# The group loop of a state-space layer: a re-ordered scan, with work moved from VectorE and GpSimd to ScalarE and back

## The chip, the cores and the metric

The kernel runs on one core of a Trainium2 chip. The metric is the device time of one execution in microseconds (us). Engines are named as in the profile: PE (TensorE), DVE (VectorE), ACT (ScalarE), POOL (GpSimd), SP (SyncE, which here only issues DMAs).

## What is computed

Two blocks of two layers each, in fp32, over 512 tokens of width 1024. Only the first layer, a Mamba-2 mixer, is touched. Per group g of 8 (4 heads of 64 each, state 128), cut to what matters:

```
z, xbc, dt = split(h @ w_in)                    # per group: 6 tiles of 128 columns
xbc = silu(conv4(xbc) + bias)                   # causal, 4 taps, per channel: x (2 tiles), B, C
for each chunk c of 128 tokens (4 chunks), head r (4 heads):
    decay = exp(min(a_cs[l] - a_cs[s], 0)), lower triangle     # a_cs: running sum of dt * A
    y  = ((C B^T) * decay) @ (x * dt)                          # inside the chunk
    y += (C * exp(a_cs)) @ state                               # from earlier chunks
    state = state * exp(a_cs[-1]) + B^T (x * dt * exp(a_cs[-1] - a_cs))
y = (y + D * x) * silu(z);   y = rmsnorm(y) @ w_out
```

## The kernel before

The whole stage lies in `ssm` (from L708). Every engine has its own queue, written out by hand; order on an engine is program order, and engines meet only at semaphores. Each product of the input projection ("piece" p of group i, L274) is 24 matmuls of 128x128 by 512 columns: 8 slices of the contraction, each in three parts, because a weight tile is split in a high part (ACT, L233, `high`) and a low part (DVE, L249, `low_on_vector`). Three split tiles are kept, so `high` and `low` run three pieces ahead.

A step i projects group i and scans group i-1. On PE (L817 on) it is: piece 0, prep 0; piece 1, out 0, prep 1; piece 2, out 1, prep 2; piece 3, out 2, prep 3; piece 4, out 3; piece 5. `prep` (L781) transposes x and B of a chunk (L789) and makes C B^T (L792). `out` (L798) makes y (L804, and L806 from the state for chunks 1 to 3) and the new state contribution (L810). A piece p waits until the result of piece p-2 has been taken out of PSUM (`lin_free`).

ACT takes pieces 0 to 3 out by a copy (L842) and pieces 4 and 5, the gates z, by Silu (L845) into `zs`; the Silu of a gate waits until the gate products of the group before (L983) are done, since `zs` is one buffer. Per chunk it copies B (L851), takes the exponential of the decay distances (L853) and, for chunks 1 to 3, of the prefix (L857). At the head of a step it does four Silus of the convolved tiles (L864).

DVE per chunk: x * dt (L947), mask of C B^T (L950), x for the state (L952), four decay distances (L956), then it waits for ACT's exponential and multiplies (L960, tile `ssm_m`); then the convolution of one tile of group i (first tap with bias L934, three taps L936), a low part (L249), and the state update (L967, L970 or, for chunk 0, L973). After chunk 3 and another low part, `gate` (L977): L981, L982, and L983, a copy to `wide`, twice. `Steps.settle` is a wait of an engine on its own last result. In the hardware loop (groups 2 to 6) such a wait is against a register.

POOL: C times exp(prefix) (L893, tile `ssm_cs`), the squares of the gated tiles (L899) and their sum (L901). SP refills the weight slots after each low part, and the prefix rows (L754) of a chunk after the chunk of the group before has used them.

After step 8, which only scans, the next block begins on PE with the sum of squares over partitions (L525).

## Time and profile before

| | |
|---|---|
| median of 3 runs | 2572.05 us (2561.34 to 2572.7) |
| profiled execution | 2570.96 us, of which span of the core 2569.0 us |
| mean granted TensorE clock | 0.930 of 2.4 GHz |
| busy, whole span | PE 89%, DVE 58%, ACT 38%, POOL 6% |
| the SSM stage (steps 0 to 8) | from about 35 us to 477 us of the span |

The profile is one execution. A line of a timeline gives start, duration, engine, source line, operation and operands, and in brackets the idle time of the engine before it and who ended it. Operations of one engine overlap by about 0.1 us, so the cost of one in a row is the difference of two starts, a little less than its duration.

### The profile page before, as it was taken

What the parts mean: (1) busy time and instruction counts of PE and PEld (TensorE: products, weight loads), DVE (VectorE), ACT (ScalarE), POOL (GpSimd) and SP (SyncE); (2) the same over time, 40 slices, a digit from 0 to 9 for tenths busy, and PEclk for the clock granted to TensorE, in tenths of its full rate; (3) what the DMA queues carried; (4) which work ended last, traced back from release to release, by engine and by line L of the source; (5) the groups of instructions that cost most, each with busy time, mean ns of one, the idle gap of its engine ahead of it and who ended that gap; (6) DMA issues with size and microseconds to landing.
All of it is one profiled execution on the core that took longest, in us unless ns stands there. A gap on an engine that the chain in (4) does not pass through costs nothing. (4 is left out here: it accounts for less than half of the span.)

```text
span 2569.0 us, 41123 instructions
## 1 busy us (share of the span) xinstructions
PE 2277.5 (89%) x15376; PEld 1969.5 (77%) x15376; DVE 1487.9 (58%) x2535; ACT 984.0 (38%) x1799; POOL 146.5 (6%) x100
## 2 busy tenths in 40 slices
PE   5988887597997779998999999989788869999998
PEld 4766665385665568885999999977666649999997
DVE  5867776635444456664566663359745445666622
ACT  4433333324444334554444432224344434434322
POOL 1021111100000000000000000022211100000000
PEclk7999998798999789997999999988999969999999
DMA  4532221133320111120233333311101102333331
GB/s 112 135 88 81 78 78 49 33 98 75 66 50 8 50 49 50 52 59 4 83 90 90 90 99 100 81 41 34 50 25 33 41 17 83 90 90 90 103 91 44
DMA packets 361091, 172.06 MB, mean 67 GB/s; under 512 B 67519, under 2 KB 359128, under 8 KB 361000
## 3 DMA queue, kind: packets, MB, share of 16 engines
q1 hardware_dynamic: 360616, 170.28, 24.1%
q0 software_dynamic: 384, 0.58, 0.2%
q8 instruction: 55, 0.90, 0.1%
q14 instruction: 36, 0.29, 0.0%
HBM read 168.68 MB, written 2.16 MB: 67 GB/s over the span
## 5 line engine op out<-in xcount | busy, mean ns | idle before, releaser
L274 PE MATMUL ps<-h_parts,parts 128*128 128x264 f32 (+1 forms) x8672 | 1353.0, 315 | 53.2 <-ACT wide L845 23.1
L274 PEld LDWEIGHTS ps<-h_parts,parts 128*128 128x128 f32 x8672 | 1208.0, 192 | 156.9 <-issue 32.3
L233 ACT ACTIVATE parts<-ring 128x1024 fp32r<-128x1024 f32 (+1 forms) x286 | 311.3, 1093 | 791.5 <-PE ps L274 544.0
L249 DVE TENSOR_TENSOR parts<-ring,parts 128x1024 fp32r<-128x1024 f32 (+1 forms) x257 | 329.5, 1288 | 251.3 <-ACT parts L233 251.1
L274 PE MATMUL ps<-wide_parts,parts 128*128 128x264 f32 (+1 forms) x1152 | 350.7, 304 | 0.0
L274 PE MATMUL ps<-up_hidden,parts 128*128 128x264 f32 x1408 | 257.9, 285 | 1.8 <-PEq L2135 1.8
L274 PEld LDWEIGHTS ps<-wide_parts,parts 128*128 128x128 f32 x1152 | 219.4, 190 | 8.0
L274 PEld LDWEIGHTS ps<-up_hidden,parts 128*128 128x128 f32 x1408 | 217.9, 188 | 2.1 <-issue 2.1
L2118 DVE TENSOR_TENSOR up_u<-ps,norm_rstd 128x264 f32<-128x264 f32 x176 | 75.4, 429 | 162.6 <-PE ps L274 155.2
L241 POOL TENSOR_TENSOR parts<-ring,parts 128x1024 fp32r<-128x1024 f32 x29 | 69.4, 2397 | 1482.2 <-ACT parts L233 1482.2
L1563 PE MATMUL ps<-wide 64*128 64x256 f32 (+5 forms) x384 | 77.3, 487 | 23.0 <-ACT wide L1700 15.8
L274 PE MATMUL ps<-gated_high,parts 128*128 128x512 f32 x256 | 85.2, 406 | 9.2 <-DVE wide_parts L298 8.2
L2385 DVE TENSOR_TENSOR res<-ps,res 128x264 f32<-128x264 f32 (+1 forms) x64 | 27.4, 432 | 102.9 <-PE ps L274 96.5
L936 DVE SCALAR_TENSOR_TENSOR ssm_conv<-wide,vec,ssm_conv 128x512 f32<-128x512 f32 x96 | 72.1, 752 | 10.1 <-DVE ssm_conv L936 0.8
L1819 DVE TENSOR_REDUCE dsa_mx<-ps 128x1 f32<-128x128 f32 (+4 forms) x80 | 42.6, 532 | 60.1 <-PE ps L1566 58.7
L2128 DVE SCALAR_TENSOR_TENSOR up_hidden_plain<-up_u,vec,up_hidden_plain 128x528 f32<-128x528 f32 x88 | 67.7, 769 | 10.3 <-DVE up_hidden_plain L2126 2.8
L2105 ACT ACTIVATE up_hidden_plain<-up_u,vec 128x528 f32<-128x528 f32 x88 | 71.7, 815 | 0.0
L274 PEld LDWEIGHTS ps<-gated_high,parts 128*128 128x128 f32 x256 | 48.8, 190 | 27.6 <-DVE wide_parts L298 8.2
L1700 ACT ACTIVATE wide<-ps,dsa_nm 128x128 f32<-128x128 f32 (+4 forms) x80 | 44.1, 556 | 65.9 <-DVE dsa_nm L1820 65.9
L1681 ACT ACTIVATE wide<-ps 128x264 f32<-128x264 f32 x80 | 31.1, 389 | 98.5 <-PE ps L274 71.0
L2126 DVE SCALAR_TENSOR_TENSOR up_hidden_plain<-up_u,vec,up_hidden_plain 128x528 f32<-128x528 f32 x88 | 66.9, 761 | 0.0
L1563 PEld LDWEIGHTS ps<-wide 64*128 64x128 f32 (+1 forms) x384 | 25.6, 166 | 48.9 <-ACT wide L1700 21.7
(294 smaller groups left out, 2549.5 us busy)
## 6 DMA issues: line engine op xcount, KB each, us to landing
ring<-in_ffn_w_up SPq DMA_DIRECT2D x88, 512.0 KB, 3.7
ring<-in_ssm_w_in SPq DMA_DIRECT2D x48, 512.0 KB, 3.9
ring<-in_ffn_w_down SPq DMA_DIRECT2D x32, 704.0 KB, 4.5
ring<-in_att_w_in SPq DMA_DIRECT2D x48, 256.0 KB, 3.6
ring<-in_da_w_qkv SPq DMA_DIRECT2D x24, 512.0 KB, 3.7
ring<-in_dsa_w_in SPq DMA_DIRECT2D x24, 512.0 KB, 3.7
ssm_prefix<-prefix_rows SPq DMA_DIRECT2D x32, 256.0 KB, 3.3
ring<-in_ssm_w_out SPq DMA_DIRECT2D x16, 512.0 KB, 4.1
```

Source lines behind the costliest of these rows:

```text
L233: self.nc.scalar.activation(self.part(st, u, 0), self.slot(u, st.kt), ACT.Copy).then_inc(self.w_high, 1)
L241: self.nc.gpsimd.tensor_tensor(self.part(st, u, 1), self.slot(u, st.kt), self.part(st, u, 0).bitcast(F32), ALU.subtract).then_inc(self.w_l ...
L249: self.nc.vector.tensor_tensor(self.part(st, u, 1), self.slot(u, st.kt), self.part(st, u, 0).bitcast(F32), ALU.subtract).then_inc(self.w_l ...
L274: m = self.nc.tensor.matmul(out, w[:, n], b, start=start and f == j == 0, stop=stop and f == st.kt - 1 and j == 2)
L936: ins = v.scalar_tensor_tensor(acc, u[:, q, j:j + SEQ], k.col(V_CW + 32 * j + tile), acc, ALU.mult, ALU.add)
L1563: m = nc.tensor.matmul(S[0:nq, x, lo:hi], rop[h, 0, c:N], rop[h, 1, lo:hi], start=True, stop=not masked)
L1700: nc.scalar.activation(p[0:nq, x, 0:c + nq], S[0:nq, x, 0:c + nq], ACT.Exp, bias=nm[0:nq, x:x + 1], scale=0.125, accum_out=den[0:nq, x:x + ...
L1819: do(v.reduce_max(mx[0:nq, x:x + 1], S[0:nq, x, 0:N], AX.X))
L2105: nc.scalar.activation(cc[:, x, :], u[:, x, 0:T2], ACT.Identity, scale=k.col(w0 + t), bias=k.col(w2 + 2 * FT + t)).then_inc(s_tap, 1)
L2118: v.tensor_tensor(u[:, x, 2 + b * HALF:2 + (b + 1) * HALF], ps[:, 2 + (2 * x + b) % 4, 0:HALF], k.rstd[:, b * HALF:(b + 1) * HALF], ALU.mu ...
L2126: v.scalar_tensor_tensor(acc, u[:, x, 1:1 + T2], k.col(w0 + 2 * FT + t), acc, ALU.mult, ALU.add).then_inc(s_mid, 1)
L2128: v.scalar_tensor_tensor(acc, u[:, x, 2:2 + T2], k.col(w2 + t), acc, ALU.mult, ALU.add).then_inc(s_conv, 1)
```

## The change

- The decay distances (`distances`) of chunk c+1 are made on DVE at the end of chunk c, those of chunk 0 at the head of the step; their exponentials and those of the prefix (`decay`, in `chunk`) follow on ACT one chunk early.
- C times exp(prefix) moves from POOL to DVE, after `ssm_m`. The state update of chunk c-1 (`carry`) moves into chunk c, between the mask and x for the state.
- The first tap of the convolution moves from DVE to ACT (`tap`), with scale and bias as columns.
- The squares move from POOL to ACT, their sum from POOL to DVE (`add_squares`), one step later; POOL has nothing left in the stage.
- `gate` writes its product straight to `wide`; the copy is gone, and `yg` is one buffer.
- ACT: `keep` copies first and then makes the high part; the gate z0 is taken out at the end of a step and waits only for the first gate product of the group before; z1 is taken out at the head of the next step; the four Silus are made at the end of the step.
- DVE: the gate follows the low part of slot 4 at once; one low part is after it, one at the head of the next step.

```diff
@@ scalar
+                def keep(i, p):
+                    act.wait_ge(sem["lin_done"], 6 * i + p + 1)
+                    wait(act, sem["conv"], 4 * i - 3 + p if not isinstance(i, int) or i else 0)
+                    nc.scalar.activation(u[:, p, 3:3 + SEQ], ps[:, p % 2, :], ACT.Copy).then_inc(sem["lin_free"], 1)
                     k.high(act, st, st.after(i, p, st.depth))
+                def tap(i, p):
+                    tile = tile_of(i, p)
+                    act.wait_ge(sem["lin_free"], 6 * i + p + 1)
+                    nc.scalar.activation(cw[:, p, :], u[:, p, 0:SEQ], ACT.Identity, scale=k.col(V_CW + tile),
+                                         bias=k.col(V_CB + tile)).then_inc(sem["tap"], 1)
+                def gates_in(i, j):
+                    act.wait_ge(sem["lin_done"], 6 * i + 5 + j)
+                    k.high(act, st, st.after(i, 4 + j, st.depth))
+                    wait(act, sem["gate"], 2 * i - 1 + j if not isinstance(i, int) or i else 0)
+                    nc.scalar.activation(zs[:, j, :], ps[:, j, :], ACT.Silu).then_inc(sem["lin_free"], 1)
+                def squares(s):
+                    for j in range(2):
+                        act.wait_ge(sem["gate"], 2 * s + j + 1)
+                        wait(act, n["accumulated"], 2 * s + b_acc + j)
+                        nc.scalar.activation(sqg[:, j, :], gated(s, j), ACT.Square).then_inc(n["squared"], 1)
+                def decay(s, c):
+                    act.wait_ge(sem["seg"], 4 * s + c + 1)
+                    nc.scalar.activation(seg[:], seg[:], ACT.Exp).then_inc(sem["dec"], 1)
                 def chunk(s, c):
+                    act.wait_ge(sem["xt"], 4 * s + c + 1)
+                    wait(act, sem["y"], 4 * s + c)
                     nc.scalar.activation(bt[:], TR[:, 2 * P:3 * P], ACT.Copy).then_inc(sem["bt"], 1)
+                    if c < CHUNKS - 1:
+                        decay(s, c + 1)
+                        wait(act, sem["cs"], 3 * s + c)
+                        act.wait_ge(s_bc[c + 1], 16 * s + 16)
+                        nc.scalar.activation(ebc[:], bc[:, c + 1], ACT.Exp).then_inc(sem["ebc"], 1)
                 def step(i, lin=True, scan=True):
                     if scan:
+                        gates_in(i - 1, 1)
+                        decay(i - 1, 0)
+                    for p in range(1, 5):
                         if lin:
+                            keep(i, p - 1)
...
+                        if lin:
+                            tap(i, p - 1)
+                        if scan:
+                            chunk(i - 1, p - 1)
+                    if lin:
+                        gates_in(i, 0)
+                        silus(i)
+                    if scan:
+                        squares(i - 1)
@@ vector, chunk
                     v.tensor_tensor(cbm[:], CB[:, 0:P], k.tri, ALU.mult).then_inc(sem["cbm"], 1)
+                    if c:
+                        carry(s, c - 1)
...
-                    dve.wait_ge(s_bc[c], 16 * s + 16)
-                    for r in range(RPG):
-                        ins = v.tensor_scalar(seg[:, r, :], bc[:, c, r, :], scal(1, c, r), 0.0, ALU.subtract, ALU.min)
-                    ins.then_inc(sem["seg"], 1)
                     dve.wait_ge(sem["dec"], n + 1)
                     dve.wait_ge(sem["cbm"], n + 1)
                     v.tensor_tensor(mm[:], seg[:], cbm[:].unsqueeze(1).to_broadcast([P, RPG, P]), ALU.mult).then_inc(sem["m"], 1)
+                    if c:
+                        dve.wait_ge(sem["ebc"], 3 * s + c)
+                        v.tensor_tensor(cs[:], ebc[:], cv[:, 3:4, c * P:(c + 1) * P].to_broadcast([P, RPG, P]), ALU.mult).then_inc(sem["cs"], 1)
+                    if c < CHUNKS - 1:
+                        dve.wait_ge(sem["m"], n + 1)
+                        distances(s, c + 1)
@@ vector, gate
                     for j in range(2):
-                        do(v.tensor_tensor(yg[:, j, :], yg[:, j, :], zs[:, j, :], ALU.mult))
-                        v.tensor_copy(k.wide[:, bass.ds(2 * s + j, 1), 0:SEQ].rearrange("p a t -> p (a t)"), yg[:, j, :]).then_inc(sem["gate"], 1)
+                        wait(dve, sem["gate"], 2 * s + j)
+                        do(v.scalar_tensor_tensor(yg[:], cv[:, j, :], k.dexp[:, bass.ds(2 * s + j, 1)], Y[j], ALU.mult, ALU.add))
+                        v.tensor_tensor(gated(s, j), yg[:], zs[:, j, :], ALU.mult).then_inc(sem["gate"], 1)
@@ vector, step
+                        distances(i - 1, 0)
+                        if lin:
+                            k.low_on_vector(dve, st, (i, 2))
+                        if squares:
+                            add_squares(i - 2)
+                    for p in range(1, 5):
                         if scan:
+                            chunk(i - 1, p - 1)
                         if lin:
+                            conv(i, p - 1)
+                            if scan or p >= 3:
+                                k.low_on_vector(dve, st, st.after(i, p - 1, st.depth))
                     if scan:
                         gate(i - 1)
                         steps.end()
                     if lin:
+                        conv_steps.end()
+                        k.low_on_vector(dve, st, st.after(i, 4, st.depth))
```

## Rows read from the trace of the kernel before

**Rows 1.** Engines in one step: stretch, length, busy (count), PE clock, DMA share, GB/s
```profile
235.00:284.00 49.00, 43.18 (x226) 33.83 (x225) 37.05 (x66) 18.07 (x28) 7.22 (x7) 0.97 0.31 85
```
**Rows 2.** Waits of PE in steps 1 to 7: total us, times, longest
```profile
PE ps L274 <- ACT wide L845: 23.1, 6, 3.9
PE ps L804 <- POOL ssm_cs L893: 21.4, 19, 1.6
```
**Rows 3.** Timeline of PE, one step: start, us, operation, [idle before]
```profile
234.72 7.38 PE L274 MATMUL ps<-h_parts,parts 128*128 128x512 f32 x24 [3.91 <-ACT wide L845]
241.94 0.49 PE L789 MATMUL ps<-cst,ssm_xbc 128*128 128x128 f32 x3
...
242.41 5.81 PE L274 MATMUL ps<-h_parts,parts 128*128 128x512 f32 x24
248.15 0.66 PE L804 MATMUL ps<-ssm_m,ssm_xdt 128*64 128x128 f32 x8
...
249.74 5.81 PE L274 MATMUL ps<-h_parts,parts 128*128 128x512 f32 x24
255.96 0.45 PE L804 MATMUL ps<-ssm_m,ssm_xdt 128*64 128x128 f32 x4 [0.40 <-POOL ssm_cs L893]
...
258.01 5.81 PE L274 MATMUL ps<-h_parts,parts 128*128 128x512 f32 x24
...
274.83 0.45 PE L804 MATMUL ps<-ssm_m,ssm_xdt 128*64 128x128 f32 x4 [1.57 <-POOL ssm_cs L893]
...
275.88 5.85 PE L274 MATMUL ps<-h_parts,parts 128*128 128x512 f32 x24
285.64 4.60 PE L274 MATMUL ps<-h_parts,parts 128*128 128x512 f32 x12 [3.91 <-ACT wide L845]
```
**Rows 4.** Windows behind such a wait, columns as in Rows 1
```profile
288.00:290.00 2.00, 2.00 (x6) 1.63 (x5) 0.63 (x2) 1.10 (x3) 0.00 (x0) 0.50 0.04 11
```
**Rows 5.** Timeline of ACT at the turn of the step
```profile
284.99 0.60 ACT L845 ACTIVATE wide<-ps 128x512 f32<-128x512 f32 x1 [9.34 <-DVE wide L983]
```
**Rows 6.** Timeline of DVE: one chunk, and the gate at the step's end
```profile
260.90 0.42 DVE L947 TENSOR_TENSOR ssm_xdt<-ps,ssm_group 128x256 f32<-128x256 f32 x1 [0.19 <-DVE ssm_state L970]
...
261.77 0.87 DVE L956 TENSOR_SCALAR ssm_seg<-ssm_prefix,ssm_group 128x128 f32<-128x128 f32 x4
263.34 0.69 DVE L960 TENSOR_TENSOR ssm_m<-ssm_seg,ssm_cb 128x512 f32<-128x512 f32 x1 [0.70 <-ACT ssm_seg L853]
...
265.68 2.54 DVE L936 SCALAR_TENSOR_TENSOR ssm_conv<-wide,vec,ssm_conv 128x512 f32<-128x512 f32 x3
268.14 1.22 DVE L249 TENSOR_TENSOR parts<-ring,parts 128x1024 fp32r<-128x1024 f32 x1
...
270.34 0.42 DVE L947 TENSOR_TENSOR ssm_xdt<-ps,ssm_group 128x256 f32<-128x256 f32 x1 [0.19 <-DVE ssm_state L970]
...
279.85 0.74 DVE L981 SCALAR_TENSOR_TENSOR ssm_yg<-ssm_xbc,dexp,ps 128x512 f32<-128x512 f32 x1
...
283.69 1.26 DVE L983 COPY wide<-ssm_yg 128x512 f32 x1
```
**Rows 7.** First tap, one line's instructions: durations in ns, min/median/max
```profile
L934 DVE TENSOR_SCALAR ssm_conv<-wide,vec x32: 541/1555/1623, 70.3 to 425.1; 128x512 f32<-128x512 f32 x32
```
**Rows 8.** The same kind of tap on ACT, in the feed-forward layer
```profile
L2105 ACT ACTIVATE up_hidden_plain<-up_u,vec x88: 809/815/820, 1282.5 to 2421.1; 128x528 f32<-128x528 f32 x88
```
**Rows 9.** Table loads of ACT in front of the exponentials, durations in ns
```profile
L853 ACT ACT_TABLE_LOAD  x8: 1283/1283/1283, 93.2 to 440.3; - x8
```
**Rows 10.** Timeline of PE before step 1 (second half is piece 0)
```profile
80.09 11.39 PE L274 MATMUL ps<-h_parts,parts 128*128 128x512 f32 x48 [1.12 <-DVE parts L249]
```
**Rows 11.** Timeline of PE in step 8 (scan only) and at the next block
```profile
438.54 0.90 PE L789 MATMUL ps<-cst,ssm_xbc 128*128 128x128 f32 x3 [5.15 <-ACT ssm_xbc L864]
...
450.76 0.70 PE L804 MATMUL ps<-ssm_m,ssm_xdt 128*64 128x128 f32 x4 [4.43 <-POOL ssm_cs L893]
...
477.30 2.04 PE L525 MATMUL ps<-norm_acc,cst 128*128 128x512 f32 x2 [8.08 <-PEq L742]
```

More of the change, by code:

```diff
@@ new lines, in gates_in, with silus @@
+                def gates_in(i, j):
[3 more added lines that the diff above has]
+                    nc.scalar.activation(zs[:, j, :], ps[:, j, :], ACT.Silu).then_inc(sem["lin_free"], 1)
+                def silus(s):
+                    wait(act, sem["gate"], 2 * s)
+                    for q in (2, 3, 0, 1):
+                        act.wait_ge(sem["conv"], 4 * s + q + 1)
+                        nc.scalar.activation(cv[:, q, :], cw[:, q, :], ACT.Silu).then_inc(sem["silu"], 1)
@@ L847, in chunk @@
                 def chunk(s, c):
-                    n = 4 * s + c
-                    act.wait_ge(sem["xt"], n + 1)
-                    wait(act, sem["y"], n)
+                    act.wait_ge(sem["xt"], 4 * s + c + 1)
+                    wait(act, sem["y"], 4 * s + c)
                     nc.scalar.activation(bt[:], TR[:, 2 * P:3 * P], ACT.Copy).then_inc(sem["bt"], 1)
-                    act.wait_ge(sem["seg"], n + 1)
-                    nc.scalar.activation(seg[:], seg[:], ACT.Exp).then_inc(sem["dec"], 1)
@@ L859, in step @@
                 def step(i, lin=True, scan=True):
                     if scan:
-                        wait(act, sem["gate"], 2 * (i - 1))
-                        for q in (2, 3, 0, 1):
-                            act.wait_ge(sem["conv"], 4 * (i - 1) + q + 1)
-                            nc.scalar.activation(cv[:, q, :], cw[:, q, :], ACT.Silu).then_inc(sem["silu"], 1)
-                    for p in range(6):
+                        gates_in(i - 1, 1)
+                        decay(i - 1, 0)
@@ L880, in _ @@
                 tables.act(act)
+                act.wait_ge(sem["group"], 1)
                 step(0, scan=False)
@@ L937, in conv, with distances @@
                         if j < 3:
-                            do(ins)
+                            conv_steps.mark(ins)
+                            conv_steps.settle(dve)
                         else:
                             ins.then_inc(sem["conv"], 1)
+                def distances(s, c):
+                    dve.wait_ge(s_bc[c], 16 * s + 16)
+                    for r in range(RPG):
+                        ins = v.tensor_scalar(seg[:, r, :], bc[:, c, r, :], scal(1, c, r), 0.0, ALU.subtract, ALU.min)
+                    ins.then_inc(sem["seg"], 1)
                 def chunk(s, c):
@@ L1018, in _ @@
                 step(0, scan=False)
-                step(1)
+                step(1, squares=False)
                 with dve.Fori(2, GROUPS - 1) as i:
```

105 lines of the change are left out of this document (25 added, 80 removed).

## The prediction

> **What bounds the kernel now.** I read the table of engines by stretch first: in one step of the loop PE is busy 43.2 of 49 us, DVE 37.1, ACT 18.1 [rows 1]. So PE is the first suspect, but not alone. The table of waits shows where it stands still: in steps 1 to 7 there are six waits of 3.9 us for the Silu that takes a gate out of PSUM, and nineteen, of up to 1.6 us, for C times decay from POOL [rows 2]. The timeline of PE then gives the step: 285.64 - 234.72 = **50.92 us**, start to start [rows 3]. The window behind the long wait shows the granted clock at 0.50, that is 1.2 GHz, in a stretch in which PE had just stood idle [rows 4], and piece 0 takes 7.22 us start to start where the others take 5.74 (248.15 - 242.41) [rows 3]: 1.5 us more per long wait.
>
> Who holds PE up? At the turn, the Silu L845 waits 9.34 us for the copy L983 at the end of DVE's gate [rows 5]. The gate lasts from 279.85 to 284.95, 5.1 us [rows 6], with the last copy stretched to 1.26 us. Inside the step DVE goes from one L947 to the next in 270.34 - 260.90 = **9.44 us**, with only 0.70 + 0.19 us idle [rows 6]. So DVE sets the pace of a chunk, and PE's wait for POOL is the shadow of it.
>
> **PE's floor.** Without its waits a step on PE is, start to start [rows 3]: slot 0, 5.74 + 0.47 (241.94 to 242.41) = 6.21; slot 1, 249.74 - 242.41 = 7.33; slots 2 and 3, 5.74 + 2.05 (255.96 to 258.01) = 7.79 each; slot 4, 5.74 + 1.05 (274.83 to 275.88) = 6.79; piece 5, 5.74. Sum **41.65 us**, 9.27 less than now. The change touches nothing on PE but a wait already met.
>
> **The new DVE slot,** c = 2, from start differences [rows 6]. Stays: L947, L950, L952, 0.87 (260.90 to 261.77). State update moved in: 270.34 - 268.14 less the low part's 1.13 = 1.07, less the settling wait of 0.19 that goes = 0.88. `ssm_m`: 0.69 less the overlap with the next, 0.61. C times decay is new here; the nearest row is `ssm_m` itself, same shape and operands, 0.61 to 0.69; I take 0.65. Distances of c+1: 0.87, I take 0.90. Three taps 265.68 to 268.14, 2.46. Low part 1.13. Sum **7.5 us** against 9.44. Gone are the first tap (265.68 - 263.34 - 0.61 = 1.73; its durations go from 0.54 to 1.62, long when POOL works beside it [rows 7]) and the wait for the exponential, 0.70. That is under PE's 7.79. It need not even be: the distance from PE's transposes to the C times decay they lead to is 0.87 + 0.88 + 0.61 + 0.69 + about 0.1 = 3.15 us, and PE has a piece of 5.74 to do meanwhile, so DVE may be 2.6 us late before PE waits.
>
> **ACT in a slot:** copy 0.5, high part 1.0, tap, B 0.3, two exponentials 1.2. The tap's price on ACT is read from the feed-forward layer: 0.815 us for 528 columns, with two column operands [rows 8]; 0.8 here. Bounds: 0.6 (ACT's plain pass, L845, [rows 5]) and 0.82. Total about 3.8 us of 7.79. The tap is queued in front of B, the exponentials and, on DVE, the three taps with a low part behind them. ACT begins it about 1.6 us after a piece ends; DVE comes to it only after the transposes (2.05) and 4.0 us of its own. So I cost it at nothing; with that cover gone it would cost 0.8 per slot, 22 us in 28 slots.
>
> On one page the rule goes against this. The Trainium skill, "ScalarE: Activation LUTs", section "Rules for kernel authors", says to put multiplies and adds on VectorE rather than ScalarE. The rows agree on the size (0.54 undisturbed against 0.8), and the sum by the rule would have the tap cost DVE 0.54 more per slot, 8.0 us, which is over PE's slot but inside DVE's lateness allowance; either way my sum stays.
>
> **The turn of the step.** Count from T, the end of piece 4. out 3 ends at T + 1.05. DVE has done its taps by then, and its low part, by T + 0.8. Gate without copies: 0.78 + 0.73, twice, plus settling: first product at T + 2.7, second at T + 4.2. The Silu of z0 needs only the first: T + 3.3. The next piece 0 starts at T + 1.05 + 5.74 = T + 6.79, so the 3.91 us wait goes with 3.5 us to spare, and with it the slow piece 0. What is late next: the low part of piece 2, at the head of the step. Its high part follows piece 5 and the squares on ACT: T + 6.8, or after four Silus (2.2) and two squares (1.2 to 1.3) behind the gate, T + 7.7, so high at T + 8.7, low at T + 9.9, two additions (0.7 each, with settling 1.7) T + 11.6. DVE's chunk 0 can begin when the transposes come, T + 6.79 + 6.1 = T + 12.9. Slack 1.3 us, and slot 0 has 1.8 more (DVE 5.7, PE 7.33). If Silu and Square called for more table loads, up to 2.6 us [rows 9], slot 0 would swallow it.
>
> DMAs: SP's queue keeps its order; each prefix refill waits for events that come earlier or in the same slot, and refills stay a group ahead. The same bytes in 42 us instead of 51 make about 100 GB/s where 85 is seen [rows 1]. Nothing; above zero would be one late weight tile of the order of the 3.9 us wait.
>
> **The sum.** Steps 1 to 7 run from the start of piece 0, 80.09 + 5.7 = 85.8 [rows 10], to 433.4 (438.54 less 5.15 [rows 11]): 347.6 us. Seven floors are 291.6. I add 0.3 us per step for hand-overs that I don't see, between 0 and 1.5 as bounds: 293.7. Gain **53.9** (45 to 56).
>
> Before step 1: the 1.12 us wait for the low part of piece 5 [rows 10] goes, since three first taps leave DVE ahead of it, 1.1.
>
> Step 8 has no pieces to hide behind; here the chain counts [rows 11]. The 5.15 us wait for the Silus goes, as they are made before piece 5 ends; instead the first exponential (z1 0.6, table load 1.3 [rows 9], Exp 0.7, `ssm_m` 0.75) comes 3.4 to 3.6 after piece 5, where `out` 0 is now 9.6 after it: 6.0. Three waits of about 4.4 hold distances, two exponentials and POOL's 1.3 one behind another; the new chain, x to C times decay, is 2.7 for chunk 1 and 3.2 for chunks 2 and 3 instead of 4.8 to 4.4: 2.0 + 1.2 + 1.2 = 4.4. From y to the next block is 8.08; new: gate 3.05, square 0.7, addition 0.8, end of block 0.5 = 5.05: 3.0. Gain **13.4** (9 to 15).
>
> In all 68.4 us. Against the profiled execution, 2570.96, it makes 2502.6; the median is 1.1 above that execution, so **2504 us**.
>
> **The rivals.**
> *DVE stays the pacemaker.* Register waits on an own result cost some 0.15 each in the loop (0.19 before L947 [rows 6]); if the new order has more of them than I count, or DVE waits for ACT's tap, a DVE slot of 8.7 makes PE late by 0.9 in three slots, 2.7 per step: + 19, 2523 us. For it: DVE's 7.5 is only 0.3 under PE's. Against: 2.6 us of lateness are allowed and the turn gives back 1.3.
> *The turn stays.* If the first gate product comes over 3.5 us later than I say, PE still waits up to 3.9 and runs at 1.2 GHz after it. 5.4 of 9.3 us per step stay: + 35, 2539 us.
> *Hand-over in series, the slower side.* ACT and DVE now feed each other twice per slot (distances to exponential, tap to taps). If neither runs ahead, a slot is 7.5 + 3.8 = 11.3 instead of 9.44, and the gate stays last: 4 x 1.9 less 1.7 for the copies = 5.9 per step, + 41, less the tail's 13: 2599 us. It decides once ACT reaches the tap over 4 us late. Against it: the one wait of this kind now is 0.70, and it lies in front of work that is moved ahead of it.
> *No visible change:* a new wait of 8 us per step in the place of the old ones, for instance a weight tile that lands late now that steps are shorter, near 2565 us.
>
> **How the numbers follow.** Forecast 0.70 (2494 to 2512), pacemaker 0.15 (2512 to 2530), turn 0.07 (2530 to 2559), no change 0.04, slower 0.04. The range 2493 to 2532 takes in the first two: about 0.85. Within 0.5% is what a measurement of this kernel can't tell from no change: faster 0.92, same 0.04, slower 0.04.
>
> **What would show it.** Right: PE steps of 41.7 to 42.5 us start to start, granted clock 1.0 throughout steps 2 to 7, no PE wait for L845's successor nor for C times decay; DVE idle at the head of the step, before the transposes; step 8 and gate to the next block in about 30 us (PE from piece 5's end to L525: 30.5 instead of 43.9). Wrong: PE waiting for `ssm_cs` or `ssm_m` in slots 2 to 4 (pacemaker), a window at clock 0.5 in each step (turn), DVE waiting for `tap` or `dec` (series), ACT's high part waiting for DMA.

## The result, and the profile after

The changed kernel takes 2489.78 us (median of 4 runs, 2486.38 to 2496.44) against 2571.77 us (2561.34 to 2572.7) for the kernel before in the same comparison: ratio 0.9693, interval [0.9661, 0.9726]. The forecast was 2504 us, in a range of 2493 to 2532. The sign was right. The time is 3.2 us under the low end: 82.0 us were gained where about 68 had been forecast.

The profiled execution took 2486.38 us. The head of its page:

```profile
span 2484.3 us, 41025 instructions
...
PE 2250.7 (91%) x15376; PEld 1952.1 (79%) x15376; DVE 1452.3 (58%) x2528; ACT 1014.6 (41%) x1847; POOL 75.5 (3%) x43
```

The next view answers to [rows 1]: engines in a whole step of the loop (stretch, length, busy and count of PE, weight loads, DVE, ACT and POOL, granted clock, DMA share, GB/s).

```profile
244.88:286.38 41.50, 41.50 (x229) 33.02 (x227) 33.03 (x65) 22.85 (x36) 0.00 (x0) 1.00 0.37 101
```

A step is now 41.50 us long, PE is busy in all of it, at a granted clock of 1.00 (2.4 GHz). Before, it was 43.2 of 49. The waits of PE in the whole stage answer to [rows 2] (total us, times, longest). None lies in steps 1 to 7:

```profile
PE ps L808 <- DVE ssm_cs L967: 7.9, 3, 2.8
...
PE ps L525 <- PEq L748: 5.0, 1, 5.0
PE ps L808 <- DVE ssm_m L964: 3.4, 1, 3.4
```

The timeline of PE answers to [rows 3]: two pieces back to back at the turn of the step (x48), then slot by slot; no bracket is left.

```profile
244.88 11.40 PE L274 MATMUL ps<-h_parts,parts 128*128 128x512 f32 x48
256.12 0.49 PE L793 MATMUL ps<-cst,ssm_xbc 128*128 128x128 f32 x3
...
279.09 0.49 PE L793 MATMUL ps<-cst,ssm_xbc 128*128 128x128 f32 x3
...
286.38 3.99 PE L274 MATMUL ps<-h_parts,parts 128*128 128x512 f32 x16
```

DVE answers to [rows 6]: one chunk, then the gate at the turn, the head of the step and the next chunk 0.

```profile
271.80 0.42 DVE L953 TENSOR_TENSOR ssm_xdt<-ps,ssm_group 128x256 f32<-128x256 f32 x1 [0.96 <-PE ps L793]
...
273.46 0.68 DVE L964 TENSOR_TENSOR ssm_m<-ssm_seg,ssm_cb 128x512 f32<-128x512 f32 x1
274.06 0.68 DVE L967 TENSOR_TENSOR ssm_cs<-ssm_ebc,ssm_xbc 128x512 f32<-128x512 f32 x1
...
275.45 2.53 DVE L934 SCALAR_TENSOR_TENSOR ssm_conv<-wide,vec,ssm_conv 128x512 f32<-128x512 f32 x3
277.90 1.22 DVE L249 TENSOR_TENSOR parts<-ring,parts 128x1024 fp32r<-128x1024 f32 x1
279.62 0.42 DVE L953 TENSOR_TENSOR ssm_xdt<-ps,ssm_group 128x256 f32<-128x256 f32 x1 [0.50 <-PE ps L793]
...
287.67 0.69 DVE L988 TENSOR_TENSOR wide<-ssm_yg,wide 128x512 f32 x1
...
294.41 1.23 DVE L249 TENSOR_TENSOR parts<-ring,parts 128x1024 fp32r<-128x1024 f32 x1 [2.07 <-ACT parts L233]
295.56 1.50 DVE L993 TENSOR_TENSOR norm_acc<-norm_acc,ssm_squares 128x512 f32<-128x512 f32 x2
298.14 0.42 DVE L953 TENSOR_TENSOR ssm_xdt<-ps,ssm_group 128x256 f32<-128x256 f32 x1 [1.09 <-PE ps L793]
```

The roles have changed: before each chunk DVE now waits for PE's transposes. ACT at the same turn answers to [rows 5]; the wait of 9.34 us for the gate is 0.63:

```profile
288.40 0.60 ACT L860 ACTIVATE wide<-ps 128x512 f32<-128x512 f32 x1 [0.63 <-DVE wide L988]
```

PE in step 8 and at the next block answers to [rows 11]:

```profile
375.06 0.54 PE L793 MATMUL ps<-cst,ssm_xbc 128*128 128x128 f32 x3
...
379.25 1.12 PE L808 MATMUL ps<-ssm_m,ssm_xdt 128*64 128x128 f32 x8 [3.42 <-DVE ssm_m L964]
...
384.93 0.45 PE L808 MATMUL ps<-ssm_m,ssm_xdt 128*64 128x128 f32 x4 [2.34 <-DVE ssm_cs L967]
...
397.99 0.70 PE L808 MATMUL ps<-ssm_m,ssm_xdt 128*64 128x128 f32 x4 [2.80 <-DVE ssm_cs L967]
...
404.99 2.04 PE L525 MATMUL ps<-norm_acc,cst 128*128 128x512 f32 x2 [5.01 <-PEq L748]
```

**Where the time went.** Three landmarks of PE's timeline cut the span: the first projection matmul of the stage, L525 (the next block's first use of the sum of squares), and the end. Before: 37.4, 477.3 and 2569.0; after: 36.1, 405.0 and 2484.3. So the start gave 1.3 us (it lies between 35.8 and 37.3 us in all the traces of this document, whatever the kernel), the stage went from 439.9 to 368.9 (**71.0 us**), and everything behind L525, in which no instruction was changed, went from 2091.7 to 2079.3 (**12.4 us**). The forecast had 68.4 for the stage and no term at all for what lies behind it.

Behind L525, the segments between further landmarks agree within half a microsecond, but for two: the sliding-window attention layer (from the end of the state-space layer's output projection to the last product with V) went from 277.5 to 271.6, the sparse attention layer from 397.4 to 390.8. In windows of the sliding-window layer laid at the same work (583 before is 511 after), first before, then after:

```profile
629.00:675.00 46.00, 44.09 (x191) 33.68 (x191) 18.30 (x26) 16.86 (x34) 0.00 (x0) 0.96 0.35 77
675.00:721.00 46.00, 42.09 (x232) 30.94 (x231) 22.43 (x35) 21.05 (x41) 0.00 (x0) 0.95 0.24 52
721.00:767.00 46.00, 44.08 (x236) 32.40 (x235) 20.70 (x34) 21.05 (x51) 0.00 (x0) 0.94 0.22 56
```

```profile
557.00:603.00 46.00, 44.09 (x198) 33.89 (x197) 19.47 (x29) 17.12 (x36) 0.00 (x0) 1.00 0.37 81
603.00:649.00 46.00, 42.09 (x240) 31.31 (x239) 22.30 (x36) 21.86 (x45) 0.00 (x0) 1.00 0.27 58
649.00:695.00 46.00, 44.08 (x248) 32.77 (x247) 22.88 (x35) 21.21 (x44) 0.00 (x0) 1.00 0.21 58
```

PE is busy for the same time and gets 27 more matmuls done, since the clock is 1.00 instead of 0.94 to 0.96. 46 us at 0.95 lose 2.3 us against 1.00, so three such windows would account for the 5.9 us of this layer and a little more. The sparse layer shows the same, first two windows of before, then the same work after:

```profile
1914.00:1964.00 50.00, 42.87 (x338) 33.19 (x337) 23.04 (x51) 21.96 (x58) 7.10 (x3) 0.96 0.11 31
1964.00:2014.00 50.00, 42.71 (x342) 32.96 (x342) 25.60 (x54) 19.56 (x58) 7.10 (x3) 0.93 0.10 25
```

```profile
1836.00:1886.00 50.00, 42.37 (x359) 32.48 (x356) 24.38 (x53) 22.00 (x60) 7.09 (x3) 1.00 0.12 31
1886.00:1936.00 50.00, 42.36 (x350) 32.13 (x349) 26.80 (x59) 21.22 (x62) 7.11 (x3) 1.00 0.11 31
```

### The profile page after: what moved, and what is told of

The parts are those of the page before. It is cut to its first block and busy times, and to the rows that moved or that the text cites. A ratio compares the mean times of both kernels' runs of the same rounds, so it can differ in the third digit from the quotient of the medians.

```text
span 2484.3 us, 41025 instructions
## 1 busy us (share of the span) xinstructions
PE 2250.7 (91%) x15376; PEld 1952.1 (79%) x15376; DVE 1452.3 (58%) x2528; ACT 1014.6 (41%) x1847; POOL 75.5 (3%) x43
## 5 line engine op out<-in xcount | busy, mean ns | idle before, releaser
L274 PE MATMUL ps<-h_parts,parts 128*128 128x264 f32 (+1 forms) x8672 | 1335.6, 312 | 28.8 <-DVE h_parts L298 16.4
L274 PEld LDWEIGHTS ps<-h_parts,parts 128*128 128x128 f32 x8672 | 1195.6, 190 | 127.0 <-issue 30.9
L274 PEld LDWEIGHTS ps<-gated_high,parts 128*128 128x128 f32 x256 | 49.0, 191 | 27.2 <-DVE wide_parts L298 7.8
```

Of the source, the lines that this page charges most:

```text
L274: m = self.nc.tensor.matmul(out, w[:, n], b, start=start and f == j == 0, stop=stop and f == st.kt - 1 and j == 2)
```

## The experiments

Two questions were open: why unchanged layers ran faster, and whether the parts of the stage's sum hold one by one. "Stage" is from the first projection matmul to L525 in the profiled execution; "outside" is the median less the stage, in which all runs count. "Sliding" and "sparse" are the two attention layers in the profiled execution. The kernel before and the changed kernel, measured first, have 439.9 and 368.9, 2131.9 and 2120.9, 277.5 and 271.6, 397.4 and 390.8 in the last four columns. All times are in us. The experiments were measured in three groups, on different chips, each beside fresh runs of the kernel before, so ratios compare better across groups than medians.

| kernel | median (n) | ratio to before | stage | outside | sliding | sparse |
|---|---|---|---|---|---|---|
| before_again | 2569.25 (10) | 0.9994 [0.9979, 1.0009] | 440.6 | 2128.7 | 277.6 | 396.8 |
| after_again | 2488.52 (4) | 0.9671 [0.9647, 0.9695] | 368.7 | 2119.8 | 275.4 | 390.8 |
| delay1 | 2495.42 (5) | 0.9705 [0.9693, 0.9718] | 369.6 | 2125.8 | 277.6 | 400.9 |
| delay4 | 2497.81 (4) | 0.9710 [0.9687, 0.9733] | 370.6 | 2127.2 | 275.8 | 396.9 |
| delay8 | 2497.91 (4) | 0.9713 [0.9689, 0.9736] | 374.3 | 2123.6 | 273.1 | 393.8 |
| before_delay | 2577.80 (11) | 1.0029 [1.0019, 1.0039] | 445.2 | 2132.6 | 277.0 | 400.0 |
| only_turn | 2529.29 (4) | 0.9842 [0.9826, 0.9859] | 401.9 | 2127.4 | 274.5 | 396.8 |
| only_tap | 2551.92 (4) | 0.9930 [0.9913, 0.9947] | 423.4 | 2128.5 | 275.5 | 396.9 |
| tap_on_vector | 2498.77 (4) | 0.9729 [0.9713, 0.9745] | 369.3 | 2129.4 | 277.0 | 394.2 |
| late_decay | 2501.15 (4) | 0.9734 [0.9718, 0.9751] | 375.9 | 2125.2 | 275.9 | 396.9 |
| cs_on_gpsimd | 2493.39 (4) | 0.9698 [0.9683, 0.9712] | 366.3 | 2127.1 | 277.7 | 396.7 |
| short_tail | 2488.66 (5) | 0.9693 [0.9677, 0.9708] | 364.7 | 2123.9 | 277.4 | 390.8 |

### The same kernels again, and the next block later

before_again and after_again are the two kernels unchanged.

> The kernel before, once more, for a second trace of it. The stage that was changed ended 72.3 us earlier in the changed kernel, but the whole span was 84.7 us shorter; 12.4 us came out of layers whose code is the same. Theory A (clock by chance): those layers take a different time from one execution to the next, since the same idle gaps of PE of about 1.9 us are followed by a stretch at 1.2 GHz in one execution and not in the other. Then this trace has the changed stage at 441 us after the first projection matmul to L525 to within 1 us (477.3 less 37.4 is 439.9), but the sliding-window layer and the sparse-attention layer differ from the first trace by some us, in steps of about 1.7. Theory B (a steady gain of the change): both layers take the same time as in the first trace to within 0.5 us, 2091.7 us from L525 to the end.

> The changed kernel, once more. Both theories: ratio 0.966 to 0.973. Theory A (clock by chance behind the stage): from L525 to the end of the span 2079 us in the first trace, here anything from 2079 to 2092, while the stage itself repeats to within 1 us (404.99 less 36.1 is 368.9). Theory B (steady gain): 2079.3 to within 1 us.

Both came back: 2569.25 (2566.68 to 2571.68) and 2488.52 (2484.69 to 2490.46). The part behind L525 was 2091.9 and 2083.0. So the extra gain is no accident of one execution; it came again with this kernel, 9 to 12 us of it by the profiles. But it is not one fixed pattern either: the kernel before repeated its two layers within 0.6 us, about as theory B had it, while in the changed kernel the sliding-window layer took 271.6 in one execution and 275.4 in another.

delay4 and delay8 put four and eight settled memsets on DVE at the end of the stage, in front of the next block. Nothing else changes; all layers behind start that much later.

```diff
                 add_squares(GROUPS - 1)
+                late = Steps(k.sem("ssm_late"))
+                for _ in range(4):
+                    late.mark(v.memset(yg[:], 0.0))
+                    late.settle(dve)
```

> The changed kernel with four dummy writes of the gate buffer on DVE, each waiting for itself, behind the last sum of squares: L525 comes 1.5 to 2 us later and nothing else is touched. Theory A (where PE's gaps fall decides the clock): the rest of the span differs from 2079.3 by up to some us either way, in the sliding-window and sparse-attention layers, with episodes at 1.2 GHz of the same length after the same gaps in some iterations and not in others. Theory B: the rest is 2079.3 and the median grows by 1.5 to 2 us.

> The same with eight dummy writes: L525 comes 3 to 4 us later. Theory A: the rest again moves by some us either way and not in proportion to the delay. Theory B: the median grows by 3 to 4 us against the changed kernel.

PE's wait in front of L525 grew from 5.01 us to 7.64 and 10.28, 0.66 us for each memset. The stage became 1.9 and 5.6 us longer than in after_again, the median 9.3 and 9.4 us. (The stage of delay4 would be 1.5 us longer but for its first part: the profiled execution had no slow stretch ahead of step 1; see "Before step 1" below.) The time outside the stage therefore rose by 7.4 and by 3.8 us, without an instruction changed there; behind L525 the profiled executions took 2090.1 and 2083.9 us, where after_again has 2083.0. Four more memsets left the median where it was. That speaks against a steady gain behind the stage and for grants that hang on when the layers run. One pair of lines shows what differs: the same place in the sliding-window layer, where PE stands idle for 1.92 us until ACT has stored the transposed scores. First before, then after:

```profile
699.50 1.90 PE L1319 MATMUL ps<-swa_pt,swa_v 128*64 128x128 f32 x16 [1.92 <-ACT swa_pt L1382]
701.33 2.81 PE L1277 MATMUL ps<-swa_raw,cst 128*128 128x512 f32 x4
```

```profile
625.67 1.09 PE L1333 MATMUL ps<-swa_pt,swa_v 128*64 128x128 f32 x16 [1.92 <-ACT swa_pt L1396]
626.69 1.98 PE L1291 MATMUL ps<-swa_raw,cst 128*128 128x512 f32 x4
```

The idle time is equal to the hundredth. Behind it the 16 matmuls take 1.90 us in one kernel and 1.09 in the other: the one is at 1.2 GHz there, the other at 2.4.

The clock records of the traces allow a count of such stretches in the middle of the sliding-window layer, from 40 to 220 us behind its start. The changed kernel's first trace has none, and the layer took 271.6 us; delay8 has one (273.1); only_turn, after_again and only_tap have two (274.5 to 275.5); delay4, late_decay, before_delay and tap_on_vector three (275.8 to 277.0); the kernel before in both traces, delay1, short_tail and cs_on_gpsimd four (277.4 to 277.7). So the differences of this layer are slow stretches that came or stayed away, and the two executions of the changed kernel differ by two of them.

delay1 has one memset, to see how little is enough. before_delay puts ten on the kernel before: if only the changed kernel were sensitive, it should cost the delay and no more.

```diff
                 step(GROUPS, lin=False)
+                late = Steps(k.sem("ssm_late"))
+                for _ in range(10):
+                    late.mark(v.memset(mm[:], 0.0))
+                    late.settle(dve)
```

> The changed kernel with one dummy write: L525 0.5 us later. Theory A: the time outside the stage depends on where the layers behind it fall to within a fraction of a microsecond (0.5 us of a longer stage in tap_on_vector went with + 9 us outside it): anything from 2120 to 2130, not 2120.5 necessarily. Theory C (what matters is the work in the stage, DVE's load above all): 2120 to 2121.

> The kernel before with ten dummy writes of ssm_m's buffer on DVE behind the last gate; the first five or six hide behind POOL's squares, so L525 comes 1.5 to 2.5 us later and the stage is 442 to 443 us. Theory A (where the later layers' gaps fall decides the clock): the time outside the stage, 2129 us in the kernel before, moves by several us, either way, as it did by + 7 with a delay of 1.8 us in the changed kernel. Theory C (the change itself leaves the later layers faster, and any delay spoils it): nothing to spoil here, 2129 to within 1.5, and the median 2572.

In delay1 L525 comes 0.66 us later behind the same work, the stage is 0.9 us longer than in after_again, and the median 6.9 us (2492.21 to 2503.17, none of its five runs as fast as the slowest of after_again, though one of the first four runs of the changed kernel, 2496.44, was as slow). The two were measured in different groups, and the interval of delay1's ratio, [0.9693, 0.9718], touches after_again's and overlaps that of the first comparison, [0.9661, 0.9726]. So a cost of so small a shift is likely, not proven; delay4 and delay8, measured beside after_again, are clear of it in every run. Its profiled execution is the slowest of the five, so its columns on the right show a bad case: the sparse layer took 400.9 us. In before_delay the stage was 445.2, 5.3 us more than in the kernel before and over the 442 to 443 expected: 4.0 in step 8, and 1.3 from a slow stretch ahead of step 1. The median rose by 7.7 against its neighbours' 2570.06. So the kernel before moves too, by 2 to 3 us outside the stage, and in the costly direction, which speaks against theory C, that a delay only spoils what the change had gained.

Over all the kernels the sparse layer took 390.8, then 393.8 and 394.2, then 396.7 to 397.4, then 400.0 and 400.9 us: steps of about 3 us. Executions with the same time mostly have the same stretches at 1.2 GHz at the same places of the layer: after, after_again and short_tail to 0.1 us, and before_again, only_turn, delay4 and late_decay to 0.3. That whole slow stretches come or stay away is shown; what in the timing decides on one of them isn't.

### The turn alone

only_turn is the kernel before with the turn of the step changed: gate before the low part, the product written to `wide` without the copy, z0 released by the first gate product.

```diff
-                        wait(act, sem["gate"], 2 * i)
+                        wait(act, sem["gate"], 2 * i + p - 5 if not isinstance(i, int) or i else 0)
...
-                        do(v.tensor_tensor(yg[:, j, :], yg[:, j, :], zs[:, j, :], ALU.mult))
-                        v.tensor_copy(k.wide[:, bass.ds(2 * s + j, 1), 0:SEQ].rearrange("p a t -> p (a t)"), yg[:, j, :]).then_inc(sem["gate"], 1)
+                        v.tensor_tensor(k.wide[:, bass.ds(2 * s + j, 1), 0:SEQ].rearrange("p a t -> p (a t)"), yg[:, j, :], zs[:, j, :], ALU.mult).then_inc(sem["gate"], 1)
...
-                        k.low_on_vector(dve, st, st.after(i, 4, st.depth))
                     if scan:
                         gate(i - 1)
                         steps.end()
                     if lin:
+                        k.low_on_vector(dve, st, st.after(i, 4, st.depth))
```

> The kernel before with the turn of the step alone: the gate product is written in place (no copy), z0 waits for the first product of the group before only, and one low part goes behind the gate. Theory 'DVE's pace': chunks stay at 9.44 us and PE's waits of 1.6 us for C times decay stay, but the wait of 3.9 us for z0 and the 1.2 GHz stretch behind it go: step 45.5 us, stage 405 us. Rival: the turn wait only moves, to the low part or the Silus of the convolved tiles; step over 48, stage over 422.

The stage fell by 38.0 us, 3 more than expected. In two steps of the loop the long wait for the gate's Silu has gone, and these are all of PE's waits (total us, times, longest):

```profile
PE ps L804 <- POOL ssm_cs L893: 7.7, 5, 1.6
PE ps L789 <- DVE ssm_group L990: 0.6, 2, 0.3
```

Over steps 1 to 7 PE waits for C times decay 15 times, 19.1 us in all, and never for a gate. So over half of the 71 us lay at the turn. The waits for C times decay stay, with DVE still the pacemaker of the chunk.

### The tap alone

only_tap is the kernel before with the first tap on ACT, behind the copy that takes the piece out.

```diff
+                        act.wait_ge(sem["lin_free"], 6 * i + p + 1)
+                        nc.scalar.activation(cw[:, p, :], u[:, p, 0:SEQ], ACT.Identity, scale=k.col(V_CW + tile),
+                                             bias=k.col(V_CB + tile)).then_inc(sem["tap"], 1)
...
-                    do(v.tensor_scalar(acc, u[:, q, 0:SEQ], k.col(V_CW + tile), k.col(V_CB + tile), ALU.mult, ALU.add))
```

> The kernel before with one part alone: the first tap on ACT, right after the copy out of PSUM. Theory 'DVE's pace': a DVE chunk falls from 9.44 to 9.44 - 1.73 = 7.7 us, under PE's 7.8, so the waits for C times decay go although that product stays on POOL (chain from the transposes 4.4 us, under a piece of 5.74); the gate, still 5.1 us behind two low parts, ends at T + 7.1 where piece 0 could start at T + 6.8, so about 1 us of the wait for z0 stays and the 1.2 GHz stretch goes. Step 42.5 us instead of 50.9; the stage, from the first projection matmul to L525, 389 us where it is 440 before and 368.8 after. Rival 'the gate must be mended by itself': the wait for z0 stays at about 3.9 us with its slow piece 0, the step is 47 us and the stage 418.

This missed: the stage is 423.4 us, 16.5 less than before; the rival had 418. The forecast's 1.73 us for the first tap, taken as DVE's saving, was the error. DVE with the tap gone:

```profile
242.18 0.69 DVE L962 TENSOR_TENSOR ssm_m<-ssm_seg,ssm_cb 128x512 f32<-128x512 f32 x1 [2.75 <-ACT ssm_seg L857]
...
257.92 0.69 DVE L962 TENSOR_TENSOR ssm_m<-ssm_seg,ssm_cb 128x512 f32<-128x512 f32 x1 [0.70 <-ACT ssm_seg L857]
258.53 3.67 DVE L938 SCALAR_TENSOR_TENSOR ssm_conv<-wide,vec,ssm_conv 128x512 f32<-128x512 f32 x3
```

and POOL beside it:

```profile
258.57 1.29 POOL L897 TENSOR_TENSOR ssm_cs<-ssm_ebc,ssm_xbc 128x512 f32<-128x512 f32 x1 [6.65 <-ACT ssm_ebc L861]
267.41 1.84 POOL L897 TENSOR_TENSOR ssm_cs<-ssm_ebc,ssm_xbc 128x512 f32<-128x512 f32 x1 [7.55 <-ACT ssm_ebc L861]
```

The three taps had taken 2.54 us [rows 6]. Now they take 3.67, because POOL's product, which starts when the exponential is there, meets them instead of the first tap. 1.1 of the 1.73 us were POOL's, and they moved on to the next instruction; the tap itself is the 0.54 us that stood as the shortest in [rows 7]. A second cost is new: in slot 0 the tap stands on ACT in front of the exponential, and DVE waits 2.75 us for it, where it waits 1.70 in the kernel before. A chunk is 8.8 us (L962 to L962, 266.76 - 257.92), with 7.7 counted on, and every turn of the loop keeps a wait of 2.4 to 3.0 us for the gate (six times, 15.0 us in all), in some with a slow piece behind it. The steps are 46.9 to 48.6 us long.

The Trainium skill, "SBUF — State Buffer", section "SBUF: two separate sides", has a rule for such a size: it calls the port pair that VectorE and GpSimd share an exclusive lock, held for a whole instruction, and counts a VectorE instruction with two SBUF inputs, as these taps are, among those that need it against a GpSimd instruction that reads SBUF. The rows agree with it: 3.67 - 2.54 = 1.13, at most the length of POOL's instruction, 1.29.

In the full change the error did no harm, since POOL's product leaves together with the tap. The turn alone (38.0 us) and the tap alone (16.5) make 54.5 of the 71 us; no run combines the two without the rest.

### The tap back on DVE, in the changed kernel

tap_on_vector undoes that part alone: DVE makes the first tap again, and PE's slot has to cover it.

```diff
-                    dve.wait_ge(sem["tap"], 4 * s + q + 1)
+                    dve.wait_ge(sem["lin_free"], 6 * s + q + 1)
+                    wait(dve, sem["silu"], 4 * s)
+                    conv_steps.mark(v.tensor_scalar(acc, u[:, q, 0:SEQ], k.col(V_CW + tile), k.col(V_CB + tile), ALU.mult, ALU.add))
```

> The changed kernel with the first tap back on DVE, as the Trainium skill's page 'ScalarE: Activation LUTs' advises for multiplies and adds. Theory 'allowance': the tap takes 0.54 plus 0.15 of settling now that POOL is quiet; DVE's chunk of 7.3 to 7.8 us becomes up to 8.0, it comes some tenths late to the third and fourth transposes and PE doesn't wait, since a late DVE has 2.6 us; step 41.5, stage 369 to 370. Rival 'DVE is at its limit': every one of 28 slots costs up to 0.7 us, stage 380 to 388.

The stage is 369.3 us, 0.4 to 0.6 more than after: DVE's lateness allowance holds, as forecast. The steps are 41.50 us long in both kernels, so in the loop the place of the tap is worth nothing; the half microsecond lies in step 8 (30.5 instead of 29.9 and 29.8), which has no taps and where the stretches at 1.2 GHz fall differently. The median nevertheless rose by 9 to 10 us, nearly all of it outside the stage (2129.4, as much as in the kernel before). Someone who compared medians alone would credit the tap with 9 us; the stage shows that it brings at most half of one.

### The exponentials late again

late_decay makes distances and exponentials of chunk c in slot c, as before, with the rest of the change left in.

```diff
-                    if c < CHUNKS - 1:
-                        decay(s, c + 1)
-                        wait(act, sem["cs"], 3 * s + c)
-                        act.wait_ge(s_bc[c + 1], 16 * s + 16)
-                        nc.scalar.activation(ebc[:], bc[:, c + 1], ACT.Exp).then_inc(sem["ebc"], 1)
+                    decay(s, c)
+                    if c:
+                        wait(act, sem["cs"], 3 * s + c - 1)
+                        act.wait_ge(s_bc[c], 16 * s + 16)
+                        nc.scalar.activation(ebc[:], bc[:, c], ACT.Exp).then_inc(sem["ebc"], 1)
```

> The changed kernel with distances and exponentials back in their own chunk (distances of chunk c behind x for the state, then the exponential, ssm_m, C times decay). Theory 'allowance': the chain from the transposes to C times decay grows from 3.1 to 4.7 us, still under a piece of 5.74, so steps stay at 41.5 us; only step 8, which has no pieces, pays: 1.2 for chunk 0 and 1.6 for each of three more, stage 375 us. Rival 'one chunk early is what made the loop fast': PE waits again for C times decay, 0.3 to 1.5 us in three slots of seven steps, stage 385 to 400.

The stage is 375.9 us, 7.0 more than in the changed kernel. PE's waits in it:

```profile
PE ps L808 <- DVE ssm_cs L968: 12.7, 3, 4.4
...
PE ps L808 <- DVE ssm_m L965: 4.7, 1, 4.7
```

All four lie in step 8 (380.29, 387.54, 396.13 and 404.72): 17.4 us where the changed kernel has 11.3. In steps 1 to 7 PE waits for nothing. So the first item of the change, exponentials one chunk early, is worth nothing in the loop, with the other parts in place, and 7 us in the one step that has no pieces to hide behind.

### C times decay back on POOL

cs_on_gpsimd takes the product from DVE and gives POOL its old loop for it; the exponentials stay early.

```diff
-                    if c:
-                        dve.wait_ge(sem["ebc"], 3 * s + c)
-                        v.tensor_tensor(cs[:], ebc[:], cv[:, 3:4, c * P:(c + 1) * P].to_broadcast([P, RPG, P]), ALU.mult).then_inc(sem["cs"], 1)
...
+                def scaled_c(s, c):
+                    pool.wait_ge(sem["ebc"], 3 * s + c)
+                    wait(pool, sem["y"], 4 * s + c)
+                    nc.gpsimd.tensor_tensor(cs[:], ebc[:], cv[:, 3:4, c * P:(c + 1) * P].to_broadcast([P, RPG, P]),
+                                            ALU.mult).then_inc(sem["cs"], 1)
```

> The changed kernel with C times decay back on POOL, where its exponential is ready a chunk early, so POOL can begin as soon as PE has used the last one. Theory 'allowance': DVE loses 0.6 of its own work per chunk and gets back about 1.1 us of blocking by POOL (the same 1.27 us product made the tap 1.0 us longer before, and the three taps of only_tap up to 1.1 longer); DVE's chunk is 7.3 to 7.9 us, PE doesn't wait, step 41.5, stage 367 to 370 us. Rival 'POOL had to go': PE waits for C times decay in three slots of seven steps, stage 378 or more.

The stage is 366.3 us, 2.6 less than in the changed kernel and a little under what was expected; the median, 2493.39, is not lower. POOL can begin as soon as PE has read the last product, a slot ahead of its use:

```profile
272.36 1.29 POOL L928 TENSOR_TENSOR ssm_cs<-ssm_ebc,ssm_xbc 128x512 f32<-128x512 f32 x1 [6.53 <-PE ps L814]
```

and what it blocks on DVE meanwhile is one instruction of the state update, which takes 0.74 us instead of 0.42 and has slack beside it. The two instructions in front of it, which read PSUM, ran beside the same product in their usual 0.42 and 0.28 us:

```profile
273.18 0.74 DVE L990 TENSOR_TENSOR ssm_statet<-ssm_state,ssm_group 128x256 f32<-128x256 f32 x1
```

So with early exponentials this move to DVE wasn't needed in the loop (the steps are 41.50 us here too), and in step 8, where DVE's chain is the path, it lengthened that chain: step 8 is 27.2 us here, 29.9 in the changed kernel.

### A shorter step 8

short_tail gives step 8 an order of its own on top of the changed kernel: C times decay ahead of x * dt, the first sum of squares later, the Silu of z1 after the scan.

```diff
+                def last_chunk(s, c):
+                    n, b4 = 4 * s + c, [P, RPG, 64]
+                    if c:
+                        dve.wait_ge(sem["y"], n)
+                        scaled_c(s, c)
...
                 def chunk(s, c):
                     n, b4 = 4 * s + c, [P, RPG, 64]
+                    if isinstance(s, int) and s == GROUPS - 1:
+                        last_chunk(s, c)
+                        if c == 0:
+                            add_squares(s - 1)
+                        return
```

> The changed kernel with step 8 alone re-ordered: ACT makes the first exponential right behind the Silus and leaves the squares of group 6 and z1 until later; DVE makes C times decay before the transposes come, the decayed state at the end of the chunk before, and x for the state behind ssm_m. Loop steps stay at 41.5. The chain of step 8 loses 1.6 at its head, 0.9 in chunk 1 and 1.4 in each of chunks 2 and 3: stage 363 to 364.5 us where it is 368.8. What the time does is another matter: with the clock of the later layers as in tap_on_vector (2128 to 2130 us outside the stage) it is 2492, with that of the changed kernel (2120) 2484.

The stage is 364.7 us, 4.0 to 4.2 less and 0.2 above what was expected. That it came so near is luck: 1.5 us of the gain lie ahead of step 1, where this execution had no slow stretch. Step 8 itself fell from 29.9 to 27.3 us, by 2.6 where 5.3 had been summed. The head gained its 1.5 (a wait of 1.90 instead of 3.42), but in chunk 1 the wait grew from 2.34 to 3.99, since the sum of squares now stands in front of it on DVE:

```profile
376.73 0.66 PE L808 MATMUL ps<-ssm_m,ssm_xdt 128*64 128x128 f32 x8 [1.90 <-DVE ssm_m L981]
...
383.19 0.70 PE L808 MATMUL ps<-ssm_m,ssm_xdt 128*64 128x128 f32 x4 [3.99 <-DVE ssm_m L981]
```

The median, 2488.66 (2488.31 to 2497.16), can't be told from the changed kernel's: the 4 us were given back outside the stage (2123.9 against 2119.8 and 2120.9). No version measured here is clearly faster than the changed kernel.

## Why the prediction was wrong, point by point

**The floor of a step.** Forecast 41.65 us, plus 0.3 for hand-overs; measured 41.50, in every step of the loop and in every variant of the changed kernel. The allowance wasn't needed. Steps 1 to 7 went from 347.6 to 290.5 us, 57.1 against 53.9 forecast. The 3.2 between are the allowance (7 x 0.3 = 2.1) and seven times 0.15.

**DVE's slot.** Forecast 7.5; measured 7.82 start to start (279.62 - 271.80), of which 0.50 is idle in front of PE's transposes: 7.3 of its own. C times decay cost 0.61 to 0.68 where 0.65 was taken. The rival in which DVE stays the pacemaker is refuted by that idle time, and its reserve is shown by tap_on_vector.

**ACT.** The tap cost 0.80 us, as read from [rows 8], and nothing on the path. The Trainium skill, "ScalarE: Activation LUTs", section "Rules for kernel authors", would have it on VectorE; tap_on_vector puts a number to that: no difference in the loop, 0.4 to 0.6 us of the stage in all. What was mis-sized is the saving on DVE, 1.73 us for a tap that takes 0.54 to 0.69 by itself; only_tap shows it, and in the full change it canceled, since the slot was summed from what stays and not from what goes.

**The turn.** The Silu of z0 began 0.63 us after ACT was free, at 288.40, and the next piece 0 had PE's wait of 3.91 us [rows 3] and its slow clock [rows 4] gone. The additions in front of chunk 0 left 1.09 us of slack (1.3 forecast). only_turn prices the turn at 38 us of stage alone.

**Before step 1.** The 1.12 us wait [rows 10] is gone, as forecast, but nothing came of it in the two traces of the changed kernel: the first transposes of step 1 come 53.9 us after the stage's start before and 54.0 after. In a window just ahead the clock fell in the changed kernel and had not before, which took the microsecond back:

```profile
64.00:69.00 5.00, 4.23 (x17) 3.44 (x18) 2.46 (x6) 1.66 (x3) 0.00 (x0) 0.66 0.02 5
```

(before, 66 to 71: 1.00). In delay4 and short_tail, with the same code up to there, the stretch stayed away and the transposes come after 52.5 us; with the tap back on DVE they come after 53.9 without it. So the forecast 1.1 was about right (1.4), and the clock took it back: the later failure in small.

**Step 8.** Forecast 13.4 us in all (9 to 15); measured 43.9 - 29.9 = 14.0. Its parts: `out` 0 comes 4.2 after the last piece instead of 9.6, 5.4 (6.0 forecast); the three waits for C times decay sum to 7.9 instead of 12.9, 5.0 (4.4 forecast); from `out` 3 to the next block 7.0 instead of 10.1, 3.1 (3.0 forecast).

**The step that failed** is one that the prediction did not write out. It made the sum of the stage against the whole profiled execution and so gave the 2091.7 us behind L525 a change of zero with no bounds. Measured, they changed by 12.4 us in the profiled pair, by 8.9 in the second pair, and by 9 to 11 in the medians. The stage's own misses are 2.6 us and would have left the forecast inside its range: 2504 less 2.6 and the 1.3 of the start is 2500. Even all upper bounds of its terms, 56 + 1.1 + 15 = 72.1, end at 2500. That the time then came to 2490 is the clock that two unchanged attention layers were granted. The prediction had a row for this mechanism, [rows 4], a stretch at 1.2 GHz behind an idle PE, and used it only inside the stage. The same view over the later layers of the kernel before shows windows of 46 to 50 us between 0.91 and 0.96, 2 to 4.5 us each that another start might free; that it can also cost more is what before_delay and delay1 show (sparse layer 400.0 and 400.9 where it had been 397.4).

How much of it belongs to the change? Outside the stage the variants of the kernel before spread over 2127.4 to 2132.6 us and those of the changed kernel over 2119.8 to 2129.4. The changed kernel stands at the fast end, and moving its next block by 2.6 us takes about 7 us away; 0.7 us of delay seems enough for 5 to 6. So 71 us (71.9 in the second pair) are the change's own, and some 10 hang on how what follows falls. That the gain turned out larger than forecast, and not smaller, is luck in this sense. Whether a few of these are steadier, since the variants of the changed kernel lie lower on average (2125 against 2130), stays open; so does what decides on a single slow stretch.

One slip of the prediction's sums touches nothing above: its rival of no visible change, 8 us per step in seven steps, makes 2504 + 56 = 2560 us and not 2565.

## What to carry to other kernels

Where a kernel has layers in which PE pauses and its clock falls, give everything behind your change a term of its own, with bounds on both sides read from the windows of the granted clock there; here it was up to 12 us of 2570, with no instruction changed there. Judge an edit by the stretch that it touches, landmark to landmark, and not by the median alone: the tap would have looked like 9 us and was at most half of one. Even a stage can hold a microsecond or two of clock, so split it again before you read a difference of that size, as short_tail teaches. And before you book an instruction's time as saved, look for its shortest duration: what stands above that belongs to a neighbour and may move to the next instruction, as POOL's 1.1 us did.

## What the runs showed of the hardware

The same 1.92 us of idle PE was followed by a stretch at 1.2 GHz in one kernel and by none in another. A delay of 2.6 us ahead of the layers cost 7 us in them, and one of 5.3 us cost 4. In the sliding-window layer none to four short slow stretches made 271.6 to 277.7 us.

POOL's product of 128x512 and a DVE tap that reads two operands from SBUF held each other up: three taps grew from 2.54 to 3.67 us beside a product of 1.29, and in the next chunk to 3.32 beside one of 1.84. Both times POOL's start is recorded 0.04 us behind the tap's, so the order of the starts doesn't tell who is held up. DVE instructions that read PSUM (0.42 and 0.28 us in cs_on_gpsimd) were not.

A table load on ACT showed no cost besides its own 1.28 us. ACT in the changed kernel, a Silu, the load and the exponential behind it:

```profile
294.29 0.57 ACT L860 ACTIVATE wide<-ps 128x512 f32<-128x512 f32 x1
294.88 1.28 ACT L876 ACT_TABLE_LOAD   x1
296.17 0.63 ACT L876 ACTIVATE ssm_seg<-ssm_seg 128x512 f32<-128x512 f32 x1
```

The load starts 0.02 us after the Silu ends, the exponential 0.01 after the load. The Trainium skill, "ScalarE: Activation LUTs", section "What ACT_TABLE_LOAD costs", gives a switch 1.38 us of drain besides the load, 2.66 in all. No such gap stands in these rows, and the measurement decides.
